# Output projection, norm, query projection and memory attention: from three stages to one, with attention worked head by head behind the queries

## The chip, the cores and the metric

The kernel runs on one core of one Trainium2 chip. That core has a matrix engine (TensorE, PE in the rows, with its weight loads as PEld), a vector engine (VectorE, DVE), an activation engine (ScalarE, ACT), a general engine (GpSimd, POOL) and a synchronising engine (SyncE, SP) that here does nothing but issue DMA transfers. Each engine runs its own instruction list in order; semaphores tie the lists together. The metric is the device time of one execution in microseconds (us); a kernel's time is the median of its runs.

## The reference, cut to what matters

One inference step of a one-layer model on 512 prompt rows and 32 sample rows, so N = 544 rows of D = 1024 features. The change lies in the middle of it: the merged mixer output `m` goes through the output projection and is added to the residual `h`; the result is normalised, projected to queries, and attends to 256 memory tokens in 4 heads of 256 features. The prompt rows and the sample rows have their own keys and values.

```python
def memory_cross_attention(u, mem_k, mem_v, wq, wo):
    B, T, _ = u.shape
    q = (u @ wq).reshape(B, T, X_HEADS, X_HEAD_DIM)
    s = jnp.einsum('bthd,bmhd->bhtm', q.astype(jnp.float32), mem_k.astype(jnp.float32)) * (X_HEAD_DIM ** -0.5)
    attn = jax.nn.softmax(s, axis=-1)
    o = jnp.einsum('bhtm,bmhd->bthd', attn, mem_v.astype(jnp.float32)).reshape(B, T, D_MODEL)
    return o.astype(u.dtype) @ wo

def trunk_layer(h, mem_k, mem_v, s_h, s_r, buf, lb, lp):
    m, s_h, s_r, buf = parallel_mixers(rmsnorm(h, lp['norm_mix_g']), s_h, s_r, buf, lb, lp)
    h = h + m @ lp['w_out']
    h = h + memory_cross_attention(rmsnorm(h, lp['norm_x_g']), mem_k, mem_v, lp['wq_x'], lp['wo_x'])
    h = h + hier_moe(rmsnorm(h, lp['norm_ffn_g']), lp)
    return h, s_h, s_r, buf
```

## The kernel before, in words

The program is a row of stages. Each is a block with one instruction list per engine, and `end_stage` closes it: the stage's semaphores are cleared and all five engines meet at a barrier, so nothing of the next stage, its DMA transfers included, is issued until the last engine of this one is done. Feature vectors lie with features on the 128 partitions: `arena` holds seven groups (H, XN, B2 to B6) of FT = 8 feature tiles, each 128 features by 544 rows. Weights come in units of 256 output columns (1 MB) into `ring`, which has two slots. `ps` is the matrix engine's output memory of 8 banks; `scr` is scratch.

Ahead of the change stands the recurrent stage (its last rows are lines up to 1732). Then come the three stages that the change merges:

1. The output projection (lines 1739 to 1768). SP loads four units of `w_out` through `linear` (line 234); POOL issues, at the same moment, the residual kept in memory (`h_kept`, 2.3 MB, line 1752) and the memory keys and values (four transfers of 1 MB, lines 1753 to 1756). PE multiplies (line 247), two feature tiles per unit; DVE adds each result to `h` (line 266).
2. The norm and the query projection (lines 1773 to 1798). ACT squares eight tiles (line 186), PE sums each over the features with a matrix of ones (line 195), ACT takes the root (line 189), DVE the reciprocal (line 203). DVE also multiplies by the gain without the norm's factor (line 201); the factor is applied to the queries as they leave the banks (line 264). Then come four units of `wq_x` through the same `linear`.
3. Memory attention by tiles of rows (lines 1803 to 1896): four tiles of 128 rows and one of 32, all four heads of a tile at once. Each tile goes ACT copy of the queries (1813), scores on PE (1848), maximum and subtraction on DVE (1834, 1838), exponential on ACT (1816), sum, reciprocal and product on DVE (1826, 1828, 1830), transposes on PE (1856), ACT copy (1818), weighted values on PE (1862), ACT copy to B3 (1820). The scores of the next tile are placed between the steps of this one.

The stage behind them (from line 1901) begins with the projection `wo_x`: SP loads its first two units at the stage's start (line 1977), PE multiplies (line 1987), and the router, the token tables and the first expert weights follow. SP issues the expert weights behind its last `wo_x` unit (line 2074), which waits for that projection's progress.

In `linear` and in attention the lists are loops; which bank or slot is free is counted by semaphores:

```python
def on_pe(pe):
    for b0, (kind, w, c0, units, x, dst) in spans:
        with pe.Fori(0, units // 2) as i:
            ...
                pe.wait_ge(S[f"banks{s}_free"], n)
                pe.wait_ge(S[f"slot{s}_loaded"], n16)
```

Of the kernel before, what the change touches and what calls it, by code (L numbers as in the profile page):

```python
# [12 lines left out]
P = 128  # L13
# [41 lines left out]
class Sems:  # L55
# [6 lines left out]
    def __getitem__(self, name):  # L62
        where = self.kept if name.startswith(("slot", "banks")) else self.by_name
# [44 lines left out]
def build(nc, I, O):  # L108
    with ExitStack() as ctx:
# [106 lines left out]
        used = [0]  # L216

        def linear(jobs):

            spans = []
            for job in jobs:
                spans.append((used[0], job))
                used[0] += job[3] // 2

            def on_sp(sp):
                for b0, (kind, w, c0, units, x, dst) in spans:
                    wv = w.rearrange("(k p) n -> p k n", p=P)
                    with sp.Fori(0, units // 2) as i:  # L230
                        n = sp.snap(i + (b0 + 1))
                        for s in range(2):
                            sp.wait_ge(S[f"slot{s}_free"], n)
                            sp.dma_start(ring[:, s], wv[:, :, bass.ds(i * (2 * UNIT) + (c0 + s * UNIT), UNIT)]).then_inc(S[f"slot{s}_loaded"], 16)

            def on_pe(pe):
                for b0, (kind, w, c0, units, x, dst) in spans:
                    with pe.Fori(0, units // 2) as i:
                        n = pe.snap(i + (b0 + 1))
                        n16 = pe.snap(i * 16 + (b0 + 1) * 16)  # L240
                        for s in range(2):
                            pe.wait_ge(S[f"banks{s}_free"], n)
                            pe.wait_ge(S[f"slot{s}_loaded"], n16)
                            for o in range(UNIT // P):
                                for h in range(2):
                                    for k in range(FT):
                                        mm = pe.matmul(ps[:, 4 * s + 2 * o + h, 0:HALF], ring[:, s, k, o * P:(o + 1) * P],  # L247
                                                       arena[:, x + k, 1 + h * HALF:1 + (h + 1) * HALF],
# [2435 lines left out]
```

## Time and profile before

| | |
|---|---|
| median of 3 runs | 1756.7 us (1754.94 to 1757.92) |
| the profiled execution: time, span of its instructions | 1759.29 us, 1757.5 us |
| PE busy, DVE busy, ACT busy | 1526.1, 647.7, 474.2 us |
| mean granted TensorE clock | 0.934 of full speed |
| from SP's first `w_out` load to PE's first `wo_x` matmul | 1060.53 to 1289.59 us |

The span runs from the first to the last instruction of the profiled execution; times in the rows count from its start. Busy shares are averages over stages with different limits, so the stretch of the three stages is read by itself. The granted clock is 1.00 at 2.4 GHz and 0.50 at 1.2 GHz. An fp32 matmul of this program stands in the trace as two records, so 128 matmuls are 256 rows of PE.

### The profile page before, as it was taken

What the parts mean: (1) busy time and instruction counts of PE and PEld (TensorE: products, weight loads), DVE (VectorE), ACT (ScalarE), POOL (GpSimd) and SP (SyncE); (2) the same over time, 40 slices, a digit from 0 to 9 for tenths busy, and PEclk for the clock granted to TensorE, in tenths of its full rate; (3) what the DMA queues carried; (4) which work ended last, traced back from release to release, by engine and by line L of the source; (5) the groups of instructions that cost most, each with busy time, mean ns of one, the idle gap of its engine ahead of it and who ended that gap; (6) DMA issues with size and microseconds to landing.
All of it is one profiled execution on the core that took longest, in us unless ns stands there. A gap on an engine that the chain in (4) does not pass through costs nothing. (4 is left out here: it accounts for less than half of the span.)

```text
span 1757.5 us, 38078 instructions
## 1 busy us (share of the span) xinstructions
PE 1526.1 (87%) x16853; PEld 1290.2 (73%) x16853; DVE 647.7 (37%) x1050; ACT 474.2 (27%) x743; POOL 231.9 (13%) x334
## 2 busy tenths in 40 slices
PE   4999997899799999989899885997689389999990
PEld 3999997788699999888888874776578355555550
DVE  4221124544536565634644631112312712222224
ACT  4232132322545565522122210101301211111111
POOL 0000001100021111100000000000010114544452
PEclk7899998999999999999999988999879589999995
DMA  4623321231722323120000006110034299999914
GB/s 154 198 74 94 96 72 50 83 121 53 242 76 74 92 82 92 31 67 4 3 3 4 3 3 233 58 61 0 0 100 168 80 368 415 363 373 381 376 55 152
DMA packets 133885, 217.84 MB, mean 124 GB/s; under 512 B 21789, under 2 KB 104214, under 8 KB 124518
## 3 DMA queue, kind: packets, MB, share of 16 engines
q1 hardware_dynamic: 108466, 175.55, 28.3%
q0 software_dynamic: 24960, 39.96, 6.6%
q8 instruction: 123, 2.02, 0.5%
q14 instruction: 28, 0.23, 0.0%
q10 hardware_dynamic: 308, 0.09, 0.0%
HBM read 249.16 MB, written 32.93 MB: 161 GB/s over the span
## 5 line engine op out<-in xcount | busy, mean ns | idle before, releaser
L319 PE MATMUL ps<-rounded,mix_hi 128*128 128x272 f32 x640 | 185.3, 290 | 17.6 <-DVE mix_lo L344 17.6
L320 PE MATMUL ps<-rounded,mix_hi 128*128 128x272 f32 x640 | 186.0, 291 | 0.0
L321 PE MATMUL ps<-rounded,mix_lo 128*128 128x272 f32 x640 | 185.4, 290 | 0.0
L2483 PE MATMUL ps<-arena,ring 128*64 128x256 f32 x1536 | 178.2, 385 | 0.0
L1049 PE MATMUL ps<-rounded,first_hi 128*128 128x272 f32 x560 | 166.0, 296 | 9.7 <-DVEq L1338 9.7
L1050 PE MATMUL ps<-rounded,first_hi 128*128 128x272 f32 x560 | 163.2, 291 | 0.0
L2483 PEld LDWEIGHTS ps<-arena,ring 128*64 128x64 f32 x1536 | 106.8, 138 | 55.2 <-issue 5.7
L247 PE MATMUL ps<-arena,ring 128*128 128x272 f32 x512 | 119.4, 395 | 20.7 <-DMA ring<-in_w_out 19.4
L319 PEld LDWEIGHTS ps<-rounded,mix_hi 128*128 128x128 f32 x640 | 121.9, 190 | 18.0 <-DVE mix_lo L344 18.0
L247 PEld LDWEIGHTS ps<-arena,ring 128*128 128x128 f32 x512 | 97.4, 191 | 42.4 <-DMA ring<-in_w_out 19.5
L321 PEld LDWEIGHTS ps<-rounded,mix_lo 128*128 128x128 f32 x640 | 122.0, 191 | 0.0
L320 PEld LDWEIGHTS ps<-rounded,mix_hi 128*128 128x128 f32 x640 | 121.6, 190 | 0.0
L1049 PEld LDWEIGHTS ps<-rounded,first_hi 128*128 128x128 f32 x560 | 107.1, 191 | 15.8 <-DVEq L1338 10.1
L344 DVE TENSOR_TENSOR mix_lo<-ring,mix_hi 128x2048 fp32r<-128x2048 f32 x20 | 45.7, 2291 | 182.6 <-ACT mix_hi L340 182.6
L1050 PEld LDWEIGHTS ps<-rounded,first_hi 128*128 128x128 f32 x560 | 106.8, 191 | 0.3
L2505 PE MATMUL ps<-arena,lora 128*64 128x512 f32 x384 | 90.6, 592 | 0.4 <-ACT lora L2533 0.4
L1051 PE MATMUL ps<-rounded,first_lo 128*128 128x272 f32 x288 | 84.3, 293 | 0.0
L1051 PE MATMUL ps<-rounded,rw_lo 128*128 128x272 f32 x272 | 78.5, 289 | 0.0
L2526 DVE TENSOR_TENSOR lora<-lora,ps 128x128 f32<-128x128 f32 x48 | 13.8, 288 | 157.5 <-ACT lora L2519 157.5
L2460 POOL DMA_INDIRECT y_slots<-arena,y_of x48 | 48.5, 1010 | 167.7 <-DVE arena L2539 126.6
L1987 PE MATMUL ps<-arena,ring 128*128 128x272 f32 x256 | 63.4, 407 | 6.4 <-DMA ring<-in_wo_x 6.4
L1987 PEld LDWEIGHTS ps<-arena,ring 128*128 128x128 f32 x256 | 49.6, 196 | 17.6 <-DMA ring<-in_wo_x 6.6
(478 smaller groups left out, 2871.2 us busy)
## 6 DMA issues: line engine op xcount, KB each, us to landing
arena<-in_expert_w_gate SPq DMA_DIRECT2D x32, 1024.0 KB, 11.7
arena<-in_expert_w_up SPq DMA_DIRECT2D x32, 1024.0 KB, 13.9
arena<-in_expert_w_down SPq DMA_DIRECT2D x32, 1024.0 KB, 11.6
ring<-in_w_in SPq DMA_DIRECT2D x20, 1024.0 KB, 5.4
ring<-in_w_in SPq DMA_DIRECT2D x35, 512.0 KB, 4.0
x_kept<-rounded POOLq DMA_DIRECT2D x2, 2176.0 KB, 15.0
rounded<-x_kept POOLq DMA_DIRECT2D x2, 2176.0 KB, 16.4
ring<-in_wk_x SPq DMA_DIRECT2D x4, 1024.0 KB, 7.0
```

Source lines behind the costliest of these rows:

```text
L247: mm = pe.matmul(ps[:, 4 * s + 2 * o + h, 0:HALF], ring[:, s, k, o * P:(o + 1) * P], arena[:, x + k, 1 + h * HALF:1 + (h + 1) * HALF], sta ...
L319: pe.matmul(out, hi[:, k], xh, start=(k == 0), stop=False)
L320: pe.matmul(out, hi[:, k], xl, start=False, stop=False)
L321: mm = pe.matmul(out, lo[:, k], xh, start=False, stop=(k == FT - 1))
L344: dve.tensor_tensor(self.lo[j], ring[:, j], self.hi[j].bitcast(F32), ALU.subtract).then_inc(S[f"w{j}_lo"], 1)
L1049: pe.matmul(out, w_hi[n % 2][:, k, :], xh, start=(k == 0), stop=False)
L1050: pe.matmul(out, w_hi[n % 2][:, k, :], xl, start=False, stop=False)
L1051: mm = pe.matmul(out, w_lo[n % 4][:, k, :], xh, start=False, stop=(k == FT - 1))
L1987: mm = pe.matmul(ps[:, 2 * (f % 2) + h, 0:HALF], ring[:, u % 2, k, (f % 2) * P:(f % 2 + 1) * P], arena[:, B3 + k, 1 + h * HALF:1 + (h + 1) ...
L2460: pool.indirect_dma_start(y_halves, block_at(i), y_b[i % 2], None, bounds_check=2 * NS - 1, oob_is_err=False).then_inc(S[f"m_y{i % 2}_out" ...
L2483: mm = pe.matmul(bank[2 + i % 2][cols[g], 0:2 * P].rearrange("t (j n) -> t j n", j=2), xT[pair % 2][:, k, cols[i % 2]], w_gu[s][:, :, k, g ...
L2505: mm = pe.matmul(bank[6 + i % 2][cols[g], :], hT[i % 2][:, k, :], w_down[s][:, k, g * 512:(g + 1) * 512], start=(k == 0), stop=(k == 1))
```

## The change

The three stages become one, without the two barriers between them, and `linear` and its loops go; all lists are written out.

- Weights: `load_projection` brings units 0 to 3 of `w_out`, 4 to 7 of `wq_x` and, in the same two slots, units 8 and 9, the first two of `wo_x`, for which the next stage's PE then has no wait. The residual is loaded by SP right behind the first unit, no longer by POOL. POOL's four loads of keys and values wait until PE has finished the first feature tile.
- Output projection and norm: DVE adds a tile to the residual, multiplies it by the gain, and sums the squares that ACT made of it; one product with ones per half, placed behind the first query tile, gives the feature sum (16 products before).
- The query projection begins when the last gain product is done; only the copying of queries out of the banks waits for the norm's factor.
- Attention goes by heads. A head needs two feature tiles of queries. Its scores for all five row tiles, its transposes and its value products are placed between the following query tiles on PE, and its maximum, exponential (now with scale, bias and running sum in the ACT instruction) and product run on DVE and ACT meanwhile. The last head has no query tile behind it.
- The value products take 512 prompt rows at once as the moving operand (4 per head, and 4 of 32 columns for the sample rows); before, 16 per row tile of 128.

```diff
+        def load_projection(sp, u):
+            if u >= 2:
+                sp.wait_ge(S["p_done"], 2 * (u - 2) + 2)
+            name, i = ("w_out", "wq_x", "wo_x")[u // 4], u % 4
...
+        def project(pe, g):
+            u, x = g // 2, (B5, XN)[g // FT]
+            if g % 2 == 0:
+                pe.wait_ge(S[f"p_w{u % 2}"], 16 * (u // 2 + 1))
+            if g >= 2:
+                pe.wait_ge(S["p_left"], g - 1)
+            if g >= FT:
+                pe.wait_ge(S["x_gained"], FT)
...
+        def scores(pe, h):
+            pe.wait_ge(S["p_left"], FT + 2 * h + 2)
...
+            for t in range(TT):
+                if h and t == 2:
+                    pe.wait_ge(S["a_kept"], h)
+                for k in range(2):
+                    mm = pe.matmul(head_tile(t), on_tokens(B2, 2 * h + k, t), kT[t // (TT - 1)][:, 2 * h + k, :], start=(k == 0), stop=(k == 1))
+            mm.then_inc(S["a_scores"], 1)
...
+        def head_exp(act, h):
+            act.wait_ge(S["a_nm"], h + 1)
+            if h:
+                act.wait_ge(S["a_turned"], h)
+            for t in range(TT):
+                m = tokens(t)
+                last = act.activation(p_s[0:m, t, :], head_tile(t)[0:m], ACT.Exp, bias=nm[0:m, t:t + 1], scale=XSCALE, accum_out=sm[0:m, t:t + 1])
+            last.then_inc(S["a_exp"], 1)
...
+        def turn_head(pe, h):
+            pe.wait_ge(S["a_p"], h + 1)
...
+        def keep_turned(act, h):
+            act.wait_ge(S["a_turned"], h + 1)
+            if h:
+                act.wait_ge(S["a_o"], h)
+            act.copy(pT[:, :, 0:SEQ], ps[:, 4:6, :])
+            act.copy(pT[:, :, SEQ:N], bank[6][:, 0:2 * DEC].rearrange("p (j n) -> p j n", j=2)).then_inc(S["a_pT"], 1)
+
+        def head_out(pe, h):
+            pe.wait_ge(S["a_pT"], h + 1)
+            if h:
+                pe.wait_ge(S["a_kept"], h)
+            for i in range(2):
+                c = slice((2 * h + i) * P, (2 * h + i + 1) * P)
+                for j in range(2):
+                    pe.matmul(bank[(7, 5)[i]], v_mem[0][:, j, c], pT[:, j, 0:SEQ], start=(j == 0), stop=(j == 1))
...
             @block.sync
             def _(sp):
-                l_sp(sp)
+                load_projection(sp, 0)
+                sp.dma_start(flat[:, H * BW:(H + FT) * BW], h_kept).then_inc(S["h_back"], 16)
+                for u in range(1, 10):
+                    load_projection(sp, u)
...
             @block.gpsimd
             def _(pool):
-                pool.dma_start(flat[:, H * BW:(H + FT) * BW], h_kept).then_inc(S["h_back"], 16)
...
+                pool.wait_ge(S["p_done"], 1)
...
             @block.tensor
             def _(pe):
-                l_pe(pe)
+                for g in range(2 * FT):
+                    project(pe, g)
+                    if g == FT:
+                        sum_features(pe)
+                    f = g - FT
+                    if f >= 4 and f % 2 == 0:
+                        head_out(pe, (f - 4) // 2)
+                    if f >= 2 and f % 2 == 0:
+                        scores(pe, (f - 2) // 2)
+                    if f >= 3 and f % 2 == 1:
+                        turn_head(pe, (f - 3) // 2)
+                head_out(pe, 2)
+                scores(pe, 3)
+                turn_head(pe, 3)
+                head_out(pe, 3)
...
             @block.vector
             def _(dve):
...
+                for f in range(FT):
+                    leave_residual(dve, f)
+                    sum_squares(dve, f)
+                dve.wait_ge(S["x_rms"], 2)
+                dve.reciprocal(q_scale, q_scale).then_inc(S["x_rrms"], 1)
+                for f in range(FT):
+                    leave_query(dve, f)
+                    if f >= 2 and f % 2 == 0:
+                        head_max(dve, (f - 2) // 2)
+                        head_scale(dve, (f - 2) // 2)
+                head_max(dve, 3)
+                head_scale(dve, 3)
...
         def project_out(pe, f):
             u = f // 2
-            if f % 2 == 0:
-                pe.wait_ge(S[f"o_w{u % 2}"], 16 * (u // 2 + 1))
+            if f % 2 == 0 and u >= 2:
+                pe.wait_ge(S[f"o_w{u % 2}"], 16)
```

SP's list at the start of the first of the three stages, before (L1745 ends the stage; each L234 pair is run twice by a loop):

```order
L234 ISA
L234 DMA ring<-in_w_out 128x8x256
L234 ISA
L234 DMA ring<-in_w_out 128x8x256
L230 REGISTER_ALU
L230 COMPARE_AND_BRANCH
L1745 UNCONDITIONAL_BRANCH
```

and of the change, from its stage's start to the next stage's first load (line numbers are now those of the changed file; L1831 ends the stage):

```order
L1695 DMA ring<-in_w_out 128x8x256
L1835 DMA arena<-h_kept 128x4624
L1695 DMA ring<-in_w_out 128x8x256 x3
L1695 DMA ring<-in_wq_x 128x8x256 x4
L1695 DMA ring<-in_wo_x 128x8x256 x2
L1831 UNCONDITIONAL_BRANCH
L2065 UNCONDITIONAL_BRANCH
L1975 DMA ring<-in_wo_x 128x8x256 x2
```

The residual has moved onto SP's queue, behind the first unit, and two `wo_x` units stand ahead of the stage's end.

PE's list in the attention stage before, a row tile of the loop (scores of the next tile, transposes, value products):

```order
L1848 MATMUL ps<-scr 128x256 x8
L1856 MATMUL ps<-ident,scr 128x128 x8
L1862 MATMUL ps<-scr 128x128 x16
L1891 REGISTER_ALU
L1891 COMPARE_AND_BRANCH
```

and of the change, from the middle of the query projection (L1708 is `project`, 16 matmuls a feature tile; L1800 `turn_head`, L1817 and L1821 `head_out`, L1765 `scores`):

```order
L1708 MATMUL ps<-arena,ring 128x272 x16
L1817 MATMUL ps<-scr 128x512 x4
L1821 MATMUL ps<-scr 128x32 x4
L1765 MATMUL ps<-scr,arena 128x256 x8
L1765 MATMUL ps<-scr,arena 32x256 x2
L1708 MATMUL ps<-arena,ring 128x272 x16
L1800 MATMUL ps<-ident,scr 128x128 x4
L1800 MATMUL ps<-ident,scr 128x32
L1800 MATMUL ps<-ident,scr 128x128 x4
L1800 MATMUL ps<-ident,scr 128x32
```

Between a head's scores and its transposes now stands one query tile; behind the last head's scores stand its transposes at once.

ACT's list of the change, from the norm's root to the end of the first head (L1858 root, L1783 exponential, L1807 and L1808 `keep_turned`, L1826 to L1828 `keep_out`); before, the table load stood in the attention loop ahead of L1813:

```order
L1858 ACTIVATE scale_row<-ps,tiny 128x272 x2
L1783 ACT_TABLE_LOAD
L1783 ACTIVATE scr<-ps,scr 128x256 x4
L1783 ACTIVATE scr<-ps,scr 32x256
L1807 COPY scr<-ps 128x2x512
L1808 COPY scr<-ps 128x2x32
L1826 COPY arena<-ps 128x512
L1827 COPY arena<-ps 128x512
L1828 COPY arena<-ps 128x2x32
```

The load now stands once, in front of the first head's exponentials, and a head takes five short activations where a row tile took one long one.

## Rows read from the trace of the kernel before

**Rows 1.** Windows: busy PE, PEld, DVE, ACT, POOL (instructions), clock, DMA share, GB/s.
```profile
1074.00:1134.40 60.40, 60.34 (x256) 49.14 (x256) 4.06 (x6) 0.00 (x0) 0.00 (x0) 0.98 0.27 97
1134.40:1147.90 13.50, 9.29 (x32) 7.11 (x33) 5.15 (x11) 5.35 (x10) 0.00 (x0) 0.87 0.48 155
1147.90:1206.90 59.00, 58.98 (x256) 48.22 (x256) 7.21 (x7) 0.00 (x0) 0.00 (x0) 1.00 0.11 36
1206.90:1283.60 76.70, 51.78 (x280) 43.70 (x280) 26.65 (x27) 22.13 (x23) 0.00 (x0) 0.85 0.00 0
```
**Rows 2.** Timeline, first stage's start: start, length, engine, line, [idle before <- what ended it].
```profile
1060.53 44.99 SPq L234 DMA_DIRECT2D ring<-in_w_out  x4
...
1073.97 60.37 PE L247 MATMUL ps<-arena,ring 128*128 128x272 f32 x256 [19.36 <-DMA ring<-in_w_out]
```
**Rows 3.** DMA issues, 1050 to 1300: median us to landing; then the ring's loads.
```profile
ring<-in_wo_x SPq DMA_DIRECT2D x2, 1024.0 KB, 5.1
...
DMA to landing us min/median/max: 4.8/5.0/13.4
```
**Rows 4.** Timeline, first matmuls of the query projection.
```profile
1147.90 2.33 PE L247 MATMUL ps<-arena,ring 128*128 128x272 f32 x9 [1.34 <-ACT scale_row L189]
```
**Rows 5.** Timeline, first row tile of attention.
```profile
1215.60 1.28 ACT L1813 ACT_TABLE_LOAD   x1 [5.42 <-PE ps L1848]
...
1216.89 1.06 ACT L1813 COPY scr<-arena 128x1024 f32 x1
...
1218.09 3.71 PE L1848 MATMUL ps<-scr 128*128 128x256 f32 x16 [2.61 <-DVE scr L1838]
...
1221.87 1.10 PE L1856 MATMUL ps<-ident,scr 128*128 128x128 f32 x8
...
1224.07 3.84 PE L1862 MATMUL ps<-scr 128*128 128x128 f32 x32 [1.10 <-ACT scr L1818]
```
**Rows 6.** Timeline, end of attention and start of the next stage.
```profile
1283.20 0.38 ACT L1820 COPY arena<-ps 128x256 f32<-128x256 f32 x1 [7.13 <-PE ps L1862]
...
1289.59 17.73 PE L1987 MATMUL ps<-arena,ring 128*128 128x272 f32 x64 [6.42 <-DMA ring<-in_wo_x]
...
1325.93 0.58 SPq L2074 DMA_DIRECT2D arena<-in_expert_w_gate  x1
```
**Rows 7.** Groups by line and shape, 1050 to 1345: busy us, mean ns of one | idle before.
```profile
L266 DVE TENSOR_TENSOR arena<-arena,ps 128x544 f32 x8 | 5.4, 718 | 71.7 <-PE ps L247 71.7
L1830 DVE TENSOR_TENSOR scr<-scr 128x1024 f32<-128x1024 f32 x4 | 4.9, 1226 | 0.1
L1834 DVE TENSOR_REDUCE scr<-ps 128x4 f32<-128x1024 f32 x4 | 4.9, 1224 | 12.0 <-PE ps L1848 11.9
L203 DVE RECIPROCAL scale_row<-scale_row 128x544 f32<-128x544 f32 x1 | 3.6, 3552 | 7.5 <-ACT scale_row L189 7.5
L201 DVE TENSOR_SCALAR arena<-arena,ca 128x544 f32<-128x544 f32 x8 | 3.4, 501 | 0.7 <-PEq L71 0.7
L189 ACT ACTIVATE scale_row<-ps,tiny 128x272 f32<-128x272 f32 x2 | 0.9, 483 | 5.6 <-PE ps L195 5.6
```
**Rows 8.** Timeline, ACT in the next stage: two copies, two activations with a running sum.
```profile
1364.10 0.58 ACT L2020 COPY scr<-ps 128x512 f32<-128x512 f32 x1 [0.96 <-PE ps L1998]
1364.58 0.25 ACT L2021 COPY scr<-ps 32x128 f32<-32x128 f32 x1
1364.86 0.42 ACT L2042 ACTIVATE arena<-scr 128x256 f32<-128x256 f32 x1
...
1365.40 0.42 ACT L2042 ACTIVATE arena<-scr 128x256 f32<-128x256 f32 x1
```
**Rows 9.** Windows as in rows 1, stretches at one clock.
```profile
1074.00:1076.60 2.60, 2.60 (x6) 2.02 (x7) 0.00 (x0) 0.00 (x0) 0.00 (x0) 0.50 1.02 411
...
1274.60:1283.60 9.00, 8.04 (x40) 7.77 (x40) 0.01 (x1) 0.75 (x2) 0.00 (x0) 0.51 0.00 0
1289.60:1294.60 5.00, 5.00 (x11) 3.84 (x12) 1.41 (x9) 0.00 (x0) 2.66 (x12) 0.50 1.08 287
```

More of the change, by code:

```diff
@@ L406, in _ @@
             def _(act):
-                for s in range(2):
-                    act.sem_inc(S[f"banks{s}_free"], 1)
                 for v, name in enumerate(VEC):
@@ L444, in _ @@
             def _(pe):
-                for s in range(2):
-                    pe.sem_inc(S[f"slot{s}_free"], 1)
                 pe.wait_ge(S["ident_ready"], 1)
@@ L1741, in build, with tokens, on_tokens @@
         v_mem = [aroom.take(2, D) for _ in range(2)]
-        l_sp, l_pe, l_leave = linear([("add", I["w_out"][0], 0, 4, B5, H)])
+        p_s, pT = aroom.take(TT, MEM), aroom.take(2, N)
+        mx, nm, sm = (aroom.take(TT) for _ in range(3))
+        square_x = [aroom.take(N) for _ in range(2)]
+        sum_x = shaped(flat, B4 * BW, (N,))
+        q_scale = scale_row[:, 0:N]
+        def tokens(t):
+            return P if t < TT - 1 else DEC
+        def on_tokens(base, f, t):
+            return arena[:, base + f, 1 + t * P:1 + t * P + tokens(t)]
@@ new lines, in sum_features, with leave_query @@
+        def sum_features(pe):
+            pe.wait_ge(S["x_summed"], FT)
+            for h in range(2):
+                mm = pe.matmul(ps[:, 4 + h, 0:HALF], ones[:, :], sum_x[:, h * HALF:(h + 1) * HALF], start=True, stop=True)
+            mm.then_inc(S["x_sums"], 1)
+        def leave_query(dve, f):
+            dve.wait_ge(S["p_done"], FT + f + 1)
+            dve.wait_ge(S["x_rrms"], 1)
+            dve.tensor_tensor(by_half(arena[:, B2 + f, 1:1 + N]), projected(f), by_half(q_scale), ALU.mult).then_inc(S["p_left"], 1)
@@ new lines, in head_out @@
+        def head_out(pe, h):
[4 more added lines that the diff above has]
+                c = slice((2 * h + i) * P, (2 * h + i + 1) * P)
+                for j in range(2):
+                    pe.matmul(bank[(7, 5)[i]], v_mem[0][:, j, c], pT[:, j, 0:SEQ], start=(j == 0), stop=(j == 1))
+            for i in range(2):
+                c = slice((2 * h + i) * P, (2 * h + i + 1) * P)
+                for j in range(2):
+                    mm = pe.matmul(bank[6][:, MEM + i * DEC:MEM + (i + 1) * DEC], v_mem[1][:, j, c], pT[:, j, SEQ:N], start=(j == 0), stop=(j == 1))
+            mm.then_inc(S["a_o"], 1)
@@ L2068, in _ @@
             def _(sp):
-                for u in range(D // UNIT):
+                for u in range(2, D // UNIT):
                     load_wo(sp, u)
```

241 lines of the change are left out of this document (81 added, 160 removed).

## The prediction

> **What bounds the stretch now.** I first read the profile's page by slices, to see where PE is less busy than in the rest of the run, and then took the stretch of the three stages apart by windows and in order of time, because a mean over the run says nothing about it. From SP's first `w_out` load to PE's first `wo_x` matmul it lasts 1289.59 - 1060.53 = 229.1 us [rows 2, 6]. PE is the engine that works almost without a break in the two projections: 60.4 us and 59.0 us for 256 records each [rows 1]. What the reader is to see beside that is four places where PE does not work. First, 13.4 us of waiting for the first unit of weights [rows 2], where a unit usually lands in about 5 us [rows 3]: the residual and the keys and values, 6.4 MB from POOL, are under way at the same time. Second, 13.5 us between the projections, of which 9.3 us are PE itself, summing squares in 32 records [rows 1, 4]. Third, attention: 76.7 us with 51.8 us of PE busy, the clock at 0.85, and PE waiting in each row tile for the steps on DVE and ACT [rows 1, 5]. Fourth, 6.4 us of waiting for `wo_x` behind the last barrier [rows 6]. Outside the projections the stretch is bound by such chains and not by any engine's work.
>
> **The first load.** Unit 0 of `w_out` now has the queues to itself; behind it on the same SP queue stand the residual and unit 1. The same pattern, two units one behind the other, gave 5.1 us for `wo_x` with router loads alongside, and 4.8 us at best [rows 3]. I take 5.1 us; the upper bound is today's 13.4 us, if the residual were served alongside. What becomes late is hidden: residual and unit 1 together are 3.3 MB, some 8 us at the 411 GB/s of [rows 9], and DVE needs the residual only after the first feature tile (7.4 us, or 59.0 / 8), PE unit 1 after two (14.8 us). POOL's 4.2 MB go out after that first tile and meet unit 2, which is asked for one tile later and needed two tiles after that: even a landing of 13.4 us is inside 14.8 us. Keys and values are needed some 60 us later.
>
> **Output projection.** 59.0 us at full clock as in the second projection [rows 1]. PE has idled before it, and idles less long now; after such idling it ran 2.6 us at 0.50 in one place and 5.0 us in another [rows 9], which costs half of that. I take 1.9 us, between 1.3 and 2.5. DVE's three passes per tile (add 0.72, gain 0.50, sum about 0.7 [rows 7]) fit many times into 7.4 us.
>
> **Handover.** PE now waits only for the last add and the last gain: 0.72 + 0.50 us [rows 7] and 0.3 us for three semaphores, 1.5 us. Before it was 13.5 us. The summing that stood there is now one product per half behind query tile 0: four records of 272 columns at the projection's 59.0 / 256 = 0.23 us, 0.9 us. The root (2 x 0.48 us), the reciprocal (3.55 us) and the first leaving of a tile (0.72 us, all [rows 7]) are 5.2 us and come while PE does query tile 1 in 7.4 us; only tile 2 needs the banks that they free.
>
> **Query projection and attention on PE.** The projection stays at 59.0 us. Scores: 10 matmuls of 256 columns per head; 8 take 3.71 us including about 0.3 us of running empty [rows 5], so 4.27 us a head, 17.1 us in all, the same columns as before. Transposes: 10 a head, 8 take 1.10 us [rows 5], 1.06 us to issue, 4.3 us in all. Values: the 4 matmuls of 512 columns are 3.41 us by the same rate per column; the 4 of 32 columns stand at the pace of a weight load, 3.84 / 32 = 0.12 us a record [rows 5], 8 records, 0.9 us: 17.4 us in all.
>
> **What a head waits for.** Between a head's scores and its transposes lie: the banks' emptying and semaphores 0.5 us; maximum 1.22 us [rows 7], the small maximum and the scaling about 0.6 us; five exponentials at the spacing of two activations with a running sum, 0.54 us [rows 8], and some 0.06 us more for a bias operand (0.48 us for 272 elements against 0.42 us for 256 [rows 7, 8]), 3.0 us; the reciprocal and the small product 0.5 us; the product 1.23 us [rows 7]. That makes 7.05 us; 6.2 us if the small pieces cost little, 9.5 us if each small piece costs like a half-size one. The cover is one query tile, 7.4 us, so heads 1 and 2 cost PE nothing, with little to spare. Behind DVE's wait for the exponentials stands only the leaving of the next query tile, which PE needs two tiles later. Head 0 also has the table load, 1.28 us, which stood behind its wait in the row of before [rows 5]; 8.3 us against 7.4 us: 1.0 us of waiting. Head 3 has no query tile behind it: PE waits 6.8 us. The step from transposes to values (an ACT copy of 1.0 us, which costs PE 1.1 us [rows 5], and a small copy) is covered by query tiles for heads 0 and 1, and is open for heads 2 and 3, 1.6 us each. The last copies out are 0.48 + 0.48 + 0.25 us [rows 8] with 0.4 us ahead of them, 1.6 us.
>
> For the table load the Trainium skill (ScalarE: Activation LUTs, What ACT_TABLE_LOAD costs) counts 1.28 us and a drain of about 1.38 us for every change of set. The row shows 1.28 us and the next instruction 0.01 us behind it, so no drain; by the skill, head 0's wait would be 2.4 us and the sum 1.4 us larger.
>
> **The clock at the end.** PE idles 6.8 us, works 1 us, idles 1.6 us, works 4.35 us. At the end of the present attention, behind similar gaps, the clock stood at 0.51 for 9 us and at 0.50 to 1294.6 [rows 9]. Work of 5.4 us at half clock costs 5.4 us more; I take 4.5 us, with 0 as the other bound. The next stage's start runs cold now and would then, no difference.
>
> **Stage end.** ACT's last copy ends at 1283.6 and PE's first `wo_x` matmul comes at 1289.6 [rows 6]; less the 5.1 us of a landing [rows 3] the barrier takes 0.9 us. The first two `wo_x` units are now already in the ring, so PE begins after those 0.9 us. The loads of expert weights stand behind the progress of this projection [rows 6], so all that follows moves with it.
>
> **Sum.** 5.1 + 60.9 + 1.5 + 59.0 + 0.9 + 17.1 + 4.3 + 17.4 + 1.0 + 1.6 + 6.8 + 1.6 + 1.6 + 4.5 + 0.9 = 184.2 us against 229.1: 44.9 us less. The profiled execution took 1759.3 us, so 1714.4 us like for like; it lies 2.6 us above the median of 1756.7, and from the median the forecast is 1711.8 us.
>
> **Rivals.** (a) The end stays warm: the clock does not fall in the last gap. For it: behind a gap of 2.6 us the scores still took only 3.71 us [rows 5]. Against it: the gap is 6.8 us. The tail saves 4.5 us and the next stage's start 2.5 us: 1704.8 us. (b) A head's chain outlasts a query tile: at 9.5 us, heads 1 and 2 wait 2.1 us each, heads 0 and 3 2.4 us more: 9 us, 1720.8 us. The cover is only 0.35 us longer than my chain, which speaks for it; that most pieces have rows speaks against it. (c) The first unit is served together with the residual and unit 1: 4.3 MB at 411 GB/s and 2 us are 12.5 us, 7.4 us more, 1719.2 us; against it stands that the first of two units on one queue landed in 4.8 to 5.1 us. (d) Slower than before: the alternation of long projections, short attention pieces and waits holds PE at half clock through the query part. Its PE work is 59.0 + 0.9 + 17.1 + 4.3 + 17.4 = 98.7 us, so all of it at half clock would add 98.7 us: 1810 us; it turns the sign from 44.9 us of such work on. Against it: the gaps ahead of head 3 are at most 1.6 us, and projections ran at 1.00 [rows 1]. The Trainium skill (TensorE: Matmul & The Clock Gate, Loop structure matters more than you think) warns that loops with a wait ahead of each burst of matmuls run cold; by that rule the query part would lean to (d). The trace agrees for the present attention, at 0.85 [rows 1]; no run here yet shows it for short waits. (e) The change gives nothing, because something later does not move with it: 1756.7 us; the row of the expert load behind this projection speaks against it.
>
> **How the numbers follow.** Forecast 62% (own range 1707 to 1717, from the cold start, the clock term and the small pieces), (a) 15%, (b) 12%, (c) 6%, (d) 3%, (e) 2%. The range takes in (a) and reaches to (b) and (c): 1703 to 1721 us. 0.2%, 3.5 us, is about what a measurement of this kernel can tell from no change; only (d) and (e) do not end faster by more: faster 95%, same 2%, slower 3%.
>
> **What would show it.** PE's first projection row should start about 5 us after SP's first load; its second about 1.5 us after the first's end; between query tiles there should be no gap over about 1 us, ahead of the last transposes one near 6.8 us; PE's first `wo_x` matmul about 1 us after ACT's last copy, and about 184 us after SP's first load. A gap ahead of the transposes of heads 1 and 2 would show (b), a first wait of over 12 us (c), a clock under 0.9 in the query part (d). The prediction is wrong if the stretch shrinks as said and the run does not, or if the copies and the small DVE pieces cost much more than their rows.

## The result and the profile after

The changed kernel takes 1707.69 us (median of 4 runs, 1706.97 to 1708.34); the kernel before, run beside it, 1757.02 us (4 runs, 1754.94 to 1757.92). The ratio is 0.9714, with a 95% interval of 0.9695 to 0.9734: 49.3 us less, where 44.9 us were forecast. The profiled execution took 1708.34 us, with a span of 1706.4 us; the mean granted clock rose from 0.934 to 0.942. Of all executions below one stands apart: one of e7's seven took 3958.99 us, for a reason that no trace shows, and is not in its ratio.

The timeline of PE after the change, from the output projection to the first `wo_x` matmul, answers to [rows 2, 4, 5, 6] (start, length, engine, line; in brackets the idle time ahead and what ended it). L1708 is the projections, L1765 scores, L1800 transposes, L1817 and L1821 the values of 512 and of 32 rows, L1985 `wo_x`:

```profile
1061.41 61.44 PE L1708 MATMUL ps<-arena,ring 128*128 128x272 f32 x256 [10.42 <-DMA ring<-in_w_out]
1124.30 7.58 PE L1708 MATMUL ps<-arena,ring 128*128 128x272 f32 x32 [1.45 <-DVE arena L1725]
...
1151.84 7.61 PE L1708 MATMUL ps<-arena,ring 128*128 128x272 f32 x32
1159.28 1.53 PE L1800 MATMUL ps<-ident,scr 128*128 128x128 f32 x10
1160.75 7.61 PE L1708 MATMUL ps<-arena,ring 128*128 128x272 f32 x32
1168.19 3.60 PE L1817 MATMUL ps<-scr 128*128 128x512 f32 x8
...
1172.43 4.68 PE L1765 MATMUL ps<-scr,arena 128*128 128x256 f32 x20
...
1197.64 4.68 PE L1765 MATMUL ps<-scr,arena 128*128 128x256 f32 x20
1202.25 7.61 PE L1708 MATMUL ps<-arena,ring 128*128 128x272 f32 x32
1209.70 1.53 PE L1800 MATMUL ps<-ident,scr 128*128 128x128 f32 x10
1212.45 3.70 PE L1817 MATMUL ps<-scr 128*128 128x512 f32 x8 [1.22 <-ACT scr L1808]
...
1227.44 2.65 PE L1800 MATMUL ps<-ident,scr 128*128 128x128 f32 x10 [5.96 <-DVE scr L1792]
1231.30 6.55 PE L1817 MATMUL ps<-scr 128*128 128x512 f32 x8 [1.22 <-ACT scr L1808]
1237.69 0.97 PE L1821 MATMUL ps<-scr 128*128 128x32 f32 x8
1240.74 16.48 PE L1985 MATMUL ps<-arena,ring 128*128 128x272 f32 x64 [2.08 <-PEq L71]
```

From the first row to 1209.70 PE stands still once, for 1.45 us. Behind that come three waits, of 1.22, 5.96 and 1.22 us, and the barrier; rows without brackets followed at once on the work ahead of them. The last transposes and values took 2.65 and 6.55 us where the heads ahead of them took 1.53 and 3.60 to 3.70.

The windows of the same stretch, which answer to [rows 1, 9] (busy time of PE, PEld, DVE, ACT and POOL with instructions, then the granted clock, DMA share and GB/s):

```profile
1061.40:1122.90 61.50, 61.44 (x256) 49.91 (x256) 13.40 (x22) 4.60 (x7) 2.61 (x6) 0.96 0.46 168
1124.30:1209.70 85.40, 85.40 (x373) 65.99 (x373) 19.50 (x27) 13.86 (x43) 0.00 (x0) 1.00 0.15 49
...
1224.00:1226.00 2.00, 0.00 (x0) 0.00 (x0) 0.29 (x2) 1.65 (x8) 0.00 (x0) 0.50 0.00 0
1232.00:1237.00 5.00, 5.00 (x7) 2.02 (x6) 0.00 (x0) 0.00 (x0) 0.00 (x0) 0.50 0.00 0
```

From 1124.30 to 1209.70 PE is busy for the whole 85.40 us at a clock of 1.00; attention before had 51.8 us of PE's work in 76.7 us at 0.85. In the 5.96 us gap the clock falls to 0.50, the lower level of 1.2 GHz, and the last values run at it.

The timelines of SP, ACT and DVE after the change give the start of the stretch, the first head's chain and ACT's last copy ([rows 2, 5, 6, 8]):

```profile
1056.28 0.38 SPq L1695 DMA_DIRECT2D ring<-in_w_out  x1
```
```profile
1153.77 1.28 ACT L1783 ACT_TABLE_LOAD   x1 [20.07 <-DVE scr L1775]
1155.06 0.47 ACT L1783 ACTIVATE scr<-ps,scr 128x256 f32<-128x256 f32 x1
1155.44 0.19 ACT L1783 ACTIVATION_READ_ACCUMULATOR scr<-ps,scr 128x1 f32 x1
1155.53 0.47 ACT L1783 ACTIVATE scr<-ps,scr 128x256 f32<-128x256 f32 x1
...
1155.98 0.47 ACT L1783 ACTIVATE scr<-ps,scr 128x256 f32<-128x256 f32 x1
...
1239.66 0.23 ACT L1828 COPY arena<-ps 128x64 f32<-128x64 f32 x1
```
```profile
1158.82 0.33 DVE L1792 TENSOR_SCALAR scr<-scr 32x256 f32<-32x256 f32 x1
```

Divided at the same events into five parts, the stretch before and after stands so ([rows 2, 4, 6] for before):

| part | before | after | forecast |
|---|---|---|---|
| first `w_out` load to PE's first matmul | 13.44 | 5.13 | 5.1 |
| output projection | 60.37 | 61.44 | 60.9 |
| handover to the query projection | 13.56 | 1.45 | 1.5 |
| query projection and attention, to ACT's last copy | 135.68 | 115.59 | 115.8 |
| last copy to the first `wo_x` matmul | 6.01 | 0.85 | 0.9 |
| sum | 229.06 | 184.46 | 184.2 |

The stretch gives 44.6 us. What the two profiled executions differ by beyond it, 51.1 - 44.6 = 6.5 us, lies outside: 4.2 us ahead of it and 2.3 us behind it (the first `wo_x` matmul to the end of the span: 467.91 us before, 465.66 after). What that is, the second profiles below tell.

### The profile page after: what moved, and what is told of

Same layout as the page of the kernel before. It is cut to its first block and busy times, and to the rows that moved or that the text cites. A ratio compares the mean times of both kernels' runs of the same rounds, so it can differ in the third digit from the quotient of the medians.

```text
span 1706.4 us, 37709 instructions
## 1 busy us (share of the span) xinstructions
PE 1507.9 (88%) x16729; PEld 1267.1 (74%) x16729; DVE 643.2 (38%) x1057; ACT 473.1 (28%) x781; POOL 232.4 (14%) x335
## 5 line engine op out<-in xcount | busy, mean ns | idle before, releaser
L1708 PE MATMUL ps<-arena,ring 128*128 128x272 f32 x512 | 121.9, 399 | 11.9 <-DMA ring<-in_w_out 10.4
L1708 PEld LDWEIGHTS ps<-arena,ring 128*128 128x128 f32 x512 | 97.7, 192 | 34.7 <-DMA ring<-in_w_out 10.6
L985 PEld LDWEIGHTS ps<-rounded,first_hi 128*128 128x128 f32 x560 | 107.1, 191 | 15.8 <-DVEq L1274 10.1
L1985 PE MATMUL ps<-arena,ring 128*128 128x272 f32 x256 | 62.1, 401 | 2.1 <-PEq L71 2.1
L291 ACT ACTIVATE arena<-ps 128x544 f32 (+1 forms) x40 | 22.8, 623 | 140.9 <-PE ps L261 140.8
```

Of the source, the lines that this page charges most:

```text
L985: pe.matmul(out, w_hi[n % 2][:, k, :], xh, start=(k == 0), stop=False)
L1708: mm = pe.matmul(ps[:, 2 * (g % 2) + h, 0:HALF], ring[:, u % 2, k, (g % 2) * P:(g % 2 + 1) * P], arena[:, x + k, 1 + h * HALF:1 + (h + 1) ...
L1985: mm = pe.matmul(ps[:, 2 * (f % 2) + h, 0:HALF], ring[:, u % 2, k, (f % 2) * P:(f % 2 + 1) * P], arena[:, B3 + k, 1 + h * HALF:1 + (h + 1) ...
```

## The experiments

"Stretch" below is always the time from SP's first `w_out` load to PE's first `wo_x` matmul, 229.06 us in the kernel before and 184.46 in the changed one. Each median stands beside runs of the kernel before on the same chip, to which the ratios go. All edits are to the changed kernel unless said.

### e1_mem_first and e2_res_pool: what made the first unit late

e1 lets POOL load keys and values at the start of the stage instead of behind the first feature tile:

```diff
-                pool.wait_ge(S["p_done"], 1)
```

> The changed kernel, but POOL issues the four loads of keys and values (4.2 MB) at the stage's start and no longer behind the first feature tile; the residual stays on SP's queue. Theory A (what held back the first weights is what shares the DMA engines with them, whatever queue it is on): PE's first matmul comes some 12 us after SP's first load, as before the change, and not 5 us, so the run is 6 to 8 us slower than the changed kernel, about 1715 us. Theory B (only the residual's 18 KB rows held it back): first matmul within 6 us, run within 2 us of the changed kernel's 1707.7.

e2 leaves that wait in place, so that keys and values still go behind the first feature tile; it issues the residual from POOL at the start of the stage instead of from SP:

```diff
-                sp.dma_start(flat[:, H * BW:(H + FT) * BW], h_kept).then_inc(S["h_back"], 16)
...
+                pool.dma_start(flat[:, H * BW:(H + FT) * BW], h_kept).then_inc(S["h_back"], 16)
                 pool.wait_ge(S["p_done"], 1)
```

> The changed kernel, but POOL issues the residual (2.3 MB) at the stage's start, beside the first unit of weights and not behind it; keys and values stay behind the first feature tile. Theory A: 2.3 MB at some 400 GB/s delay the first unit by up to 5.8 us; first matmul 8 to 11 us after SP's first load, run 3 to 6 us slower, about 1712 us. Theory C (one queue serves its loads in order, two queues in turns by row, so big rows win): the full 5.8 us. If the first matmul still comes after 5 us, where the residual stands does not matter: 1707.7 us.

e1 took 1709.4 us (ratio 0.9716, 0.9697 to 0.9735), e2 1708.54 us (0.9708, 0.9691 to 0.9724). PE's first matmul came 5.17 us behind the load in e1 and 5.23 us in e2, as in the changed kernel. PE's timeline in e1 shows who paid instead, and the landings of the ring's loads with it:

```profile
1060.43 17.37 PE L1708 MATMUL ps<-arena,ring 128*128 128x272 f32 x64 [10.46 <-DMA ring<-in_w_out]
1080.07 44.31 PE L1708 MATMUL ps<-arena,ring 128*128 128x272 f32 x192 [2.27 <-DMA ring<-in_w_out]
```
```profile
DMA to landing us min/median/max: 5.0/5.1/23.7
```

Unit 1, not unit 0, landed late, after 23.7 us, and PE waited 2.27 us for it. In e1 the same 6.4 MB as in the kernel before were asked for at the start, 4.2 MB of them on POOL's queue and the residual on SP's behind unit 0; in e2 POOL's queue had the residual with its rows of 18 KB, as before, but only these 2.3 MB. Unit 0 landed in about 5.2 us in both, and theory A fails in both. So neither 4.2 MB on POOL's queue nor the residual's rows there are by themselves enough for the 13.4 us [rows 3] that the forecast laid to POOL's bytes under way at the same time; all 6.4 MB on POOL's queue were tried in neither run. What also differed from the kernel before was the start of the two queues: there POOL's first issue stood 0.13 us behind SP's, in e1 and e2 0.45 to 0.47 us. The packets of the first 4.0 us behind SP's first issue (queue, packets, MB, share of 16 engines; q1 is SP's queue) show what that did, in e1 and then in e2:

```profile
q1 hardware_dynamic: 895, 0.92, 74.7%
```
```profile
q1 hardware_dynamic: 866, 0.89, 65.1%
```

POOL's queue (q0) had moved nothing yet, and most of unit 0's 1024 packets were through; so e2 did not yet put theory C's turns to the test. That led to e7.

### e7_before_late_pool: the first unit in the kernel before

One line in the kernel **before**, at the start of POOL's list for the output projection, so that its queue starts later:

```diff
+                pool.memset(scr[:, 10000:12048], 0.0)
                 pool.dma_start(flat[:, H * BW:(H + FT) * BW], h_kept).then_inc(S["h_back"], 16)
```

> The kernel before, with one instruction more: in the output projection's stage POOL fills 2048 columns of dead scratch before it issues its first transfer, so that its queue starts some 1.9 us later (a fill of 1024 columns took 0.95 to 0.97 us in the kernel before); nothing else is changed, the same bytes are asked for. Theory P (the two queues are served packet for packet once both have work, so that what counts is how much of the first weight unit is through before POOL's packets start): unit 0 lands about 5.1 us after its issue instead of 13.4, PE's first matmul comes about 8 us earlier, unit 1 now meets POOL's packets and costs PE up to about 3 us once, and the kernel is 5 to 8 us faster than before (about 1750). Theory B (the bytes in flight beside the load set its landing, whatever came first): unit 0 still lands after 11 to 13 us and the time is within 2 us of before.

It took 1749.33 us against 1756.55 (ratio 0.995, 0.993 to 0.9971): 7.2 us faster by one line that computes nothing. POOL's first issue now stands 1.43 us behind SP's instead of 0.13. The stretch is 222.30 us. Its PE timeline and SP's, where 5.13 us have taken the place of the 13.44 of before:

```profile
1060.50 37.39 SPq L234 DMA_DIRECT2D ring<-in_w_out  x4
...
1065.63 61.08 PE L247 MATMUL ps<-arena,ring 128*128 128x272 f32 x256 [11.04 <-DMA ring<-in_w_out]
```

The queues' packets in the first 4.0 us after SP's issue (queue, packets, MB, share of 16 engines; q1 is SP's queue, whose rows of weights are 1 KB each, q0 POOL's), in the kernel before and then in e7:

```profile
q1 hardware_dynamic: 637, 0.65, 49.5%
q0 software_dynamic: 22, 0.41, 24.6%
```
```profile
q1 hardware_dynamic: 956, 0.98, 75.6%
```

and in the 4.0 us behind that in the kernel before:

```profile
q0 software_dynamic: 90, 1.66, 97.4%
q1 hardware_dynamic: 87, 0.09, 6.3%
```

Unit 0 is 1024 packets. In e7 956 were through before POOL had moved one. In the kernel before 637 were, and from there on both queues got about the same number of packets, 87 and 90, although POOL's are some 18 KB each and SP's 1 KB: the remaining 387 rows of weights waited behind big neighbours one by one. In the 6 us behind that POOL's packets were of 4 to 6 KB and the turns came quicker, 377 against 381. Theory P holds and theory B falls: the bytes and their queues are those of the kernel before, and only the start of POOL's queue moved. The projection behind it saw no second wait; of the 8.3 us gained at the start, 6.8 remained in the stretch. The rest is matmuls that took other times in the two profiles: the output projection 0.7 us and attention 2.5 us more in e7, the sums of the norm 1.7 us less.

### e3_no_preload: the first two `wo_x` units

They are loaded by the next stage again, as before:

```diff
-                for u in range(1, 10):
+                for u in range(1, 8):
...
-                for u in range(2, D // UNIT):
+                for u in range(D // UNIT):
```

> The changed kernel without the two wo_x units ahead of the stage's end; the next stage loads them at its start as before the change. Theory of the forecast: PE's first wo_x matmul comes 5.1 us later, the clock there stays low for longer, run 5 to 7 us slower, about 1713.5 us. Rival (the next stage's start is set by the router's loads and tables, so PE's earlier start is only given back as a wait later in that stage): run within 2 us of 1707.7.

1713.11 us (ratio 0.9731, 0.9715 to 0.9748), the stretch 189.70. PE's timeline:

```profile
1245.05 5.34 PE L1986 MATMUL ps<-arena,ring 128*128 128x272 f32 x12 [7.30 <-DMA ring<-in_wo_x]
```

7.30 us of waiting stand where 2.08 stood: 5.2 us. The medians differ by 5.4 us from the changed kernel and by 4.6 from e2 on the same chip, but the ratios' intervals overlap, so the row carries this. The early load is worth its 5.2 us, as the last row of the table above has it.

### e4_heads_after: all query tiles first, then the heads

```diff
-                    f = g - FT
-                    if f >= 4 and f % 2 == 0:
-                        head_out(pe, (f - 4) // 2)
...
+                for h in range(XH):
+                    scores(pe, h)
+                    turn_head(pe, h)
+                    head_out(pe, h)
```

(and the same on DVE). 

> The changed kernel with the same instructions, but all eight query tiles first and the four heads one after the other behind them, so that no query tile covers a head's softmax. Theory of the forecast (cover is what counts): heads 0 to 2 each wait about 6 us more for the softmax and 1.2 us for the copy of the transposes, and the clock falls in those gaps, so that scores and values run at half for part of the time: 22 us and 6 to 20 us of clock, run 25 to 40 us slower, 1733 to 1748 us. Rival (the gain of the attention came from fewer barriers, fewer instructions and the wider value products, not from the cover): less than 12 us slower, under 1720 us.

1733.75 us (ratio 0.9860, 0.9836 to 0.9883), the stretch 212.94. The window of attention:

```profile
1182.00:1265.40 83.40, 53.32 (x186) 32.76 (x184) 14.24 (x25) 18.79 (x58) 0.00 (x0) 0.75 0.04 13
```

Attention by heads without cover takes 83.4 us at a clock of 0.75, longer than attention by row tiles before (76.7 us at 0.85 [rows 1]). Each head waits 5.96 to 7.30 us for its product and 1.22 us for its copy. So working by heads gains nothing in itself; that each head's chain lies behind a query tile gives 26.1 us of the change's 49.3 by the medians, 28.5 in the stretch: the largest single part. It was forecast as a sum of pieces and is here measured as one.

### e5_warm_tail and e6_last_early: the 5.96 us ahead of the last transposes

e5 fills the gap with 12 matmuls of the ones matrix whose results nobody reads:

```diff
                 scores(pe, 3)
+                for i in range(12):
+                    pe.matmul(bank[0][:, 0:HALF], ones[:, :], arena[:, XN, 1:1 + HALF], start=True, stop=True)
                 turn_head(pe, 3)
```

> The changed kernel with twelve extra matmuls (5.5 us, into a bank that nothing reads any more) while PE waits for the last head's softmax; the outputs do not change. Theory of the forecast (the gap lets the clock fall, which makes the last transposes and values take twice their time): transposes 1.5 us and values 3.6 us as for the other heads, not 2.65 and 6.55 us, and the next stage starts at full clock: 4 to 6 us faster, about 1702.5 us. Rival (the last values are slow for another reason, the freshly written operand or the banks): values still 6.5 us, run the same as the changed kernel.

1704.73 us (ratio 0.9707, 0.9688 to 0.9726), the stretch 180.70, 3.8 us less by useless work. The times show it less clearly: 3.0 us by the medians, and the ratios' intervals overlap. PE's timeline:

```profile
1220.06 5.77 PE L1881 MATMUL ps<-arena,ones 128*128 128x272 f32 x24
1226.10 1.59 PE L1800 MATMUL ps<-ident,scr 128*128 128x128 f32 x10 [0.26 <-DVE scr L1792]
1228.90 3.70 PE L1817 MATMUL ps<-scr 128*128 128x512 f32 x8 [1.22 <-ACT scr L1808]
```

Transposes and values are back at 1.59 and 3.70 us: the half clock in the tail cost (2.65 - 1.59) + (6.55 - 3.70) = 3.9 us, where 4.5 were forecast. The next stage did not start at full clock, as had been expected: its first `wo_x` unit took 16.60 us, against 16.48 in the changed kernel.

That cost is not fixed by the gaps. In e1 the last head has the same waits, 5.96 and 1.22 us, and yet the last values took 5.28 us, and the first `wo_x` unit ran at full clock without any filler:

```profile
1240.99 14.92 PE L1984 MATMUL ps<-arena,ring 128*128 128x272 f32 x64 [2.08 <-PEq L71]
```

There the tail's half clock cost 2.6 us. The second profile of the changed kernel, and that of e2, have 6.5 and 16.5 us like the first; why e1 differs is not shown.

e6 fills it with useful work: the last head's scores go ahead of the third head's values, into banks of their own (0 to 2, free once the last queries have left):

```diff
-            return bank[4 + t // 2][:, (t % 2) * MEM:(t % 2 + 1) * MEM] if t < TT - 1 else bank[6][0:DEC, 0:MEM]
+            b0 = 0 if h == XH - 1 else 4
+            return bank[b0 + t // 2][:, (t % 2) * MEM:(t % 2 + 1) * MEM] if t < TT - 1 else bank[b0 + 2][0:DEC, 0:MEM]
...
-                head_out(pe, 2)
                 scores(pe, 3)
+                head_out(pe, 2)
                 turn_head(pe, 3)
```

ACT likewise does the last head's exponentials ahead of the third head's copies out.

> The changed kernel with the last head's scores ahead of the head before's value products, in the banks that the query projection has left free, so that those value products cover part of the last softmax. Theory of the forecast (the chain of the last head, 6 us of waiting, and the low clock behind it are what is left of the stage): PE waits about 2 us ahead of the last transposes instead of 6, and not 1.2 us ahead of head 2's values; the clock stays up; 8 to 11 us faster, about 1698 us. Rival (ACT becomes the bound, since it must put the last exponentials between two heads' copies): under 4 us faster.

1701.27 us (ratio 0.9678, 0.9659 to 0.9698), the stretch 177.71, 6.7 us less, and not the 8 to 11 that had been expected. PE's timeline:

```profile
1225.33 1.59 PE L1803 MATMUL ps<-ident,scr 128*128 128x128 f32 x10 [1.52 <-DVE scr L1793]
1228.14 6.47 PE L1820 MATMUL ps<-scr 128*128 128x512 f32 x8 [1.22 <-ACT scr L1811]
...
1237.50 16.44 PE L1993 MATMUL ps<-arena,ring 128*128 128x272 f32 x64 [2.08 <-PEq L71]
```

The long wait shrank from 5.96 to 1.52 us, but the values still took 6.47: gaps of 1.52 and 1.22 us around 1.59 us of transposes were followed by the lower clock as well (0.50 from 1227.00 to 1228.10).

### e9_early_warm, e10_small_warm and e6_again: both together

e9 puts fillers into the gaps that e6 left, 12, 10 and 16 of them:

```diff
                 head_out(pe, 2)
+                warm(pe, 12)
                 turn_head(pe, 3)
+                warm(pe, 10)
                 head_out(pe, 3)
+                warm(pe, 16)
```

> e6_last_early (the last head's scores ahead of the third head's values) with matmuls of the ones matrix, whose results nobody reads, put into the three gaps of PE that remained: 12 after the third head's values, 10 after the last head's transposes, 16 after the last head's values (0.11 us each at full clock). Theory C (what remained in the tail of e6_last_early was half clock in the last values, 6.5 against 3.7 us, and in the next stage's first unit, 16.5 to 16.6 against 14.4): the last values take 3.7, the stretch loses 2.5 to 3 us and the time comes to 1697 to 1699; if the clock also survives the barrier, the first wo_x unit takes about 14.5 and another 2 us go. Theory N (the fillers cost what they save, since they stand in PE's queue ahead of the awaited work): within 1 us of e6_last_early's 1701.3.

1709.15 us (ratio 0.973, 0.9711 to 0.975): 7.9 us slower than e6 by the medians. PE's timeline says why:

```profile
1217.95 5.75 PE L1829 MATMUL ps<-arena,ones 128*128 128x272 f32 x24
...
1229.68 3.60 PE L1820 MATMUL ps<-scr 128*128 128x512 f32 x8
...
1242.34 14.92 PE L2000 MATMUL ps<-arena,ring 128*128 128x272 f32 x64 [0.84 <-PEq L71]
```

The clock stayed up (values 3.60, first `wo_x` unit 14.92 instead of 16.44), but twelve fillers are 24 records of 0.24 us, 5.75 us in a gap of 1.52. The size of one, 0.48 us, had stood in e5's row; the expectation had it wrong. e10 has fewer:

```diff
-                warm(pe, 12)
+                warm(pe, 3)
...
-                warm(pe, 10)
+                warm(pe, 2)
...
-                warm(pe, 16)
+                warm(pe, 2)
```

> e9_early_warm with fewer fillers: 3, 2 and 2 instead of 12, 10 and 16. In e9_early_warm a filler took 0.48 us (24 rows of 0.24 for 12), not the 0.11 that its expectation was worked out with, so that they overran the gaps of 1.52, 1.22 and about 2 us that they stood in; the clock did stay up (last values 3.60, first wo_x unit 14.92). Theory C, re-sized (3 x 0.48 = 1.44, 2 x 0.48 = 0.96, 2 x 0.48 = 0.96 fit into the gaps): last values 3.6 to 3.7, first wo_x unit 15 to 16.5, the stretch 174.5 to 175.5 instead of 177.7 in e6_last_early, the time 1697 to 1699. Theory N (short fillers don't hold the clock, or delay what stands behind them by as much as they save): the last values stay near 6.5 and the time within 1 us of e6_again, measured beside it.

> The kernel of e6_last_early once more, on the same chip and beside e10_small_warm: 1701 to 1702, stretch 177.5 to 178.

e10 took 1697.56 us (ratio 0.9663, 0.965 to 0.9676), e6_again beside it 1700.25 us (0.968, 0.9667 to 0.9694). The stretch is 174.94 against 177.72 us. PE's timeline of e10, and a window over the last values:

```profile
1217.96 1.62 PE L1829 MATMUL ps<-arena,ones 128*128 128x272 f32 x6
1219.64 1.59 PE L1803 MATMUL ps<-ident,scr 128*128 128x128 f32 x10
1221.16 1.18 PE L1829 MATMUL ps<-arena,ones 128*128 128x272 f32 x4
1222.45 3.70 PE L1820 MATMUL ps<-scr 128*128 128x512 f32 x8
...
1229.04 14.92 PE L2000 MATMUL ps<-arena,ring 128*128 128x272 f32 x64 [1.08 <-PEq L71]
```
```profile
1223.00:1228.00 5.00, 4.96 (x20) 2.77 (x18) 0.00 (x0) 1.00 (x3) 0.00 (x0) 1.00 0.00 0
```

With seven matmuls without a use the clock stood at 1.00 through the tail and into the next stage: 2.8 us in the stretch, and the first `wo_x` unit took 14.92 us instead of 16.42 in e6_again. That these 1.5 us are the fillers' doing is not shown: e1 and e4 had 14.92 without a filler. By the medians it is 2.7 us; the two ratios' intervals overlap, so the rows carry this more than the times do. e10 is the fastest version found, 10.1 us below the changed kernel by the medians and 0.5% by the ratios.

### before_again and after_again: the rest of the gain

Both kernels once more, unchanged, for a second profile of each.

> The kernel before, unchanged, for a second profile. The recurrent stage ended 3.6 us later in the profile of the kernel before than in that of the changed kernel, with the same code up to there; 2.9 us of it in the first norm, where PE's sums took 10.5 us and 7.6 us. Theory L (the clock's state at that moment differs between executions): the first norm's sums take anything from 7.5 to 10.5 us. Theory M (it belongs to the program): 10.5 us again.

> The changed kernel, unchanged, for a second profile. Theory L: the first norm's sums take anything from 7.5 to 10.5 us, and the next stage's first matmuls are at full clock after a varying time. Theory M: 7.6 us again. The stretch from SP's first load to PE's first wo_x matmul: 184.5 us within 2 us in both.

They took 1753.66 and 1706.87 us, 46.8 us apart, with stretches of 229.03 and 184.42 us: 44.6 us again. The sums of the first norm, at the very start of the program, far ahead of the change, in the timelines of before, after and before_again:

```profile
19.56 10.50 PE L195 MATMUL ps<-scr,ones 128*128 128x272 f32 x32 [2.41 <-ACT scr L186]
```
```profile
19.55 7.57 PE L195 MATMUL ps<-scr,ones 128*128 128x272 f32 x32 [2.12 <-ACT scr L186]
```
```profile
18.38 7.57 PE L195 MATMUL ps<-scr,ones 128*128 128x272 f32 x32 [2.41 <-ACT scr L186]
```

The same instructions took 10.50 us in one execution of the kernel before and 7.57 in another. So most of the 4.2 us ahead of the stretch, in the first pair of profiles, differs from execution to execution and is no effect of the change; in the second pair only 0.5 us lie there. These do look like the change's: SP's first `w_out` load is issued 5.25 us behind its last store before and 4.62 us after, and the same two gaps stand in the first pair. Behind the stretch the second pair has 1.9 us, the first 2.3. What the change itself gives, by the profiles, is thus 44.6 + about 2 + about 0.5 = 47 us; the medians' 49.3 has an interval, from the ratio's, of 46.7 to 53.6 us.

## Why the prediction was right

**The first load: right in size, wrong in cause.** 5.13 us against 5.1. The forecast laid the 13.4 us to 6.4 MB under way at the same time, and rival (c) would have had the residual and unit 1 delay unit 0 in the changed kernel too. e1 has the same 6.4 MB under way, on other queues, and 5.17 us; e7 keeps the same bytes on the same queues, only starts POOL's queue later, and has 5.13 us. The order in which queues start, and that packets of 1 KB take turns with packets of 18 KB, made the 13.4. In the changed kernel POOL waits for the first feature tile, so its queue cannot begin beside unit 0. Most of this part, 8.3 us of the gain, could be had from the kernel before with one line: e7 was 7.2 us faster by the medians.

**Output projection and handover.** 61.44 against 60.9 us: the cold start took the clock's mean to 0.96 and cost 2.4 us, more than the 1.9 us allowed for and inside its bounds of 1.3 to 2.5. 1.45 against 1.5 us: the add and the gain of the last tile, as worked out. The 13.5 us of the norm went behind the next tiles, and no wait appears there.

**Query projection and attention: 115.59 against 115.8, by errors that cancelled.** PE's work at full clock came out larger than the forecast: a query tile 7.45 us (1202.25 to 1209.70) against 7.4, scores 4.61 (1197.64 to 1202.25) against 4.27, transposes 1.47 (1159.28 to 1160.75) against 1.06, values 4.24 (1168.19 to 1172.43) against 4.35; with the norm's 0.9 that is 8 x 7.45 + 0.9 + 4 x (4.61 + 1.47 + 4.24) = 101.8 us against 98.7. The subtracted "0.3 us of running empty" and the issue time of the transposes were the mis-sized terms. The waits came out smaller: head 0 waited 0 instead of 1.0 us, the copies cost 1.22 instead of 1.6 twice, the last head's chain 5.96 instead of 6.8: 8.4 us against 11.0. The clock in the tail cost 3.9 us against 4.5, and the last copies 1.2 against 1.6. That the sum comes within 0.2 us is luck: PE's work was 3.1 us too small in it and the waits, the clock and the copies together 3.6 us too large; some 0.3 us of the 115.59 lie in none of these rows.

Most of what makes the chain shorter shows in one kind of row: exponentials with a running sum follow each other every 0.45 to 0.47 us (1155.06, 1155.53, 1155.98), because the reading of the accumulator, 0.19 us, overlaps the next one; the forecast had 0.60, from 0.54 for another kind of operand and a supplement. Five of them are 2.3 us, not 3.0. Head 0's chain, its table load included, ran from 1151.84 to the product's end at 1159.15 us and the cover to 1159.28: it fits by about 0.1 us. Rival (b) was that near for head 0.

The table load stood at 1153.77 for 1.28 us, and the next instruction came 0.01 us behind it. The Trainium skill (ScalarE: Activation LUTs, What ACT_TABLE_LOAD costs) counts a drain of about 1.38 us more for each change of set; this trace shows none. By an estimate from that page's figure, head 0 would have waited some 1.2 us with one.

**The stage's end.** 0.85 against 0.9 us, and 5.2 us for the preload in e3, both as forecast.

**The rivals.** (a), a tail that stays warm, did not happen, and e5 and e10 show what it would have been: 3.9 us in the tail (4.5 forecast), and at most 1.5 us in the first `wo_x` unit (2.5 forecast), which e5 did not get. (d), half clock through the query part, is refuted by 85.40 us at 1.00: with no wait ahead of any of it, work in pieces of 1.0 to 14.8 us ran at full clock throughout. The Trainium skill's warning (TensorE: Matmul & The Clock Gate, Loop structure matters more than you think) is of a long DMA wait ahead of every matmul; the prediction left the length out. In kind it agrees with e4, where the waits of 5.96 to 7.30 us were for DVE and attention ran at 0.75.

**What the forecast missed** lies outside its sum: it let nothing change behind the stretch, "runs cold now and would then, no difference". The first unit of `wo_x` took 17.73 us before [rows 6] and 16.48 after, and 2 us in all were gained there; and the profiled execution of before lost 3 us at its start, which the change has no part in.

## What to carry to other kernels

A chain of steps on other engines is best hidden by interleaving it with long PE work whose length is known, but compare chain and cover row by row: here it fitted by 0.1 us, and the one head without cover set the tail. When a first load lands late, look at which queue starts first and at the size of each queue's rows before blaming the bytes; shifting one issue by 1.3 us against the other queue's gave 7 us here. Short gaps ahead of the last work of a stage cost twice here, in the wait and in the clock behind it: move the last chain forward first, and fill what remains with no more work than the gap is long.

## What the runs showed of the hardware

- Two DMA queues with work each got about one packet in turn, whatever its size: 87 packets of 1 KB against 90 of 18 KB in 4 us (0.09 and 1.66 MB, kernel before). SP's queue alone moved 374 of the small packets in one us.
- The clock fell to 0.50 behind gaps of 1.52 and 1.22 us around 1.59 us of transposes (e6), and stayed at 1.00 when 1.62 and 1.18 us of matmuls stood in these gaps (e10). That filler matmuls kept the tail at full clock is shown (e5, e10); that they sped up the next stage's start is not, and from what gap on the clock falls was not tried. The changed kernel's gaps of 5.96 and 1.22 us were followed by 6.5 us of values in four profiles of the change's tail (both of the changed kernel, e2, e3) and by 5.28 us in e1.
- The same matmuls at the program's start took 7.57 us in most executions, 9.05 in one and 10.50 to 10.60 in three, and differed between two of the same kernel: a difference of 3 us between two profiles need not be the change's.
